# Feed-forward feature products with rounded and rest activations side by side, 512 columns per matmul

## The reference

```python
# block 1, each layer (D_FF = 4096)
h2 = rms_norm(x, mlp_norm_g[l])
x = x + jnp.square(jax.nn.relu(h2 @ w_up[l])) @ w_down[l]

# block 2, each layer, twice (ffn1 and ffn2; D_FF_2 = 2816)
def _swiglu(x, w1, w3, w2):
    return (jax.nn.silu(x @ w1) * (x @ w3)) @ w2
x = _layer_norm(a * x + 0.5 * _swiglu(x, ffn1_w1[l], ffn1_w3[l], ffn1_w2[l]), ln1_g[l], ln1_b[l])
```

## Time and profile before

| | us |
|---|---|
| median of 3 runs (lowest to highest) | 2394.6 (2394.44 to 2394.92) |
| the profiled execution | 2392.54 |
| its span, first to last instruction | 2390.8 |
| granted TensorE clock, mean | 0.990 |

### The profile page before, as it was taken

One profiled execution on the slowest core, in us unless ns is written; L12 is line 12 of the kernel. 1 busy time (PEld: TensorE's weight loads), 2 busy tenths in 40 slices (PEclk: granted clock), 3 DMA queues, 4 the chain that ended last, 5 costly groups with the idle time before them and its releaser, 6 DMA issues.

```text
span 2390.8 us, 38487 instructions
## 1 busy us (share of the span) xinstructions
PE 2311.5 (97%) x16084; PEld 2123.2 (89%) x16098; DVE 1353.6 (57%) x1782; ACT 1152.1 (48%) x1797; POOL 186.9 (8%) x191
## 2 busy tenths in 40 slices
PE   7999999999999999999999999999999999998998
PEld 6988988888998998799998889989988999897997
DVE  4556555646664545655566665465555555776454
ACT  4754544674553444545443544454444445355443
POOL 0001210001110210000003001111100000110110
PEclk9999999999999999999999999999999999999999
DMA  6324555432555655554533545565555444263554
GB/s 223 132 97 152 184 197 181 163 121 97 190 189 185 222 182 189 171 181 141 168 106 110 190 156 181 191 208 188 187 174 184 155 158 143 80 205 134 184 178 146
DMA packets 109005, 395.93 MB, mean 166 GB/s; under 512 B 12374, under 2 KB 12544, under 8 KB 108576
## 3 DMA queue, kind: packets, MB, share of 16 engines
q1 hardware_dynamic: 104400, 377.53, 47.7%
q0 software_dynamic: 4432, 15.93, 2.2%
HBM read 392.92 MB, written 1.05 MB: 165 GB/s over the span
## 4 chain that ended last, share of the span: by engine, by line
PE 89%; DVE 5%; ACT 3%; DMA 1%; issue 1%; SPq 0%; DVEq 0%; ACTq 0%
PE psum L390 80%; PE psum L805 2%; PE psum L771 2%; DVE w_low L347 2%; PE psum L707 2%; DMA ring<-in_weights 1%; PE psum L789 1%; ACT w_high L344 1%; ACT attn_p L887 1%; PE psum L1773 1%; DVE mx L831 1%; DVE xT_low L666 0%; PE psum L1113 0%; ACT xT_high L660 0%; PE psum L1101 0%
## 5 line engine op out<-in xcount | busy, mean ns | idle before, releaser
L347 DVE TENSOR_TENSOR w_low<-ring,w_high 128x1024 fp32r<-128x1024 f32 x704 | 863.5, 1255 | 577.3 <-ACT w_high L344 575.7
L344 ACT ACTIVATE w_high<-ring 128x1024 fp32r<-128x1024 f32 x704 | 718.0, 1052 | 302.1 <-DMA ring<-in_weights 301.5
L390 PE MATMUL psum<-xT_high,w_high 128*128 128x256 f32 x2976 | 848.0, 285 | 0.0
L390 PE MATMUL psum<-xT_low,w_high 128*128 128x256 f32 x2976 | 843.3, 283 | 0.0
L390 PE MATMUL psum<-xT_high,w_low 128*128 128x256 f32 x2976 | 843.2, 283 | 0.0
L390 PEld LDWEIGHTS psum<-xT_high,w_high 128*128 128x128 f32 x2976 | 572.6, 192 | 0.8
L390 PEld LDWEIGHTS psum<-xT_low,w_high 128*128 128x128 f32 x2976 | 572.6, 192 | 0.4
L390 PEld LDWEIGHTS psum<-xT_high,w_low 128*128 128x128 f32 x2976 | 572.3, 192 | 0.0
L390 PE MATMUL psum<-w_high,hidden 128*128 128x512 f32 x1216 | 376.6, 390 | 0.0
L390 PEld LDWEIGHTS psum<-w_high,hidden 128*128 128x128 f32 x1216 | 228.3, 188 | 47.1
L390 PE MATMUL psum<-w_low,hidden 128*128 128x512 f32 x608 | 236.6, 389 | 0.0
(11 more groups left out here) (233 smaller groups left out, 2196.0 us busy)
## 6 DMA issues: line engine op xcount, KB each, us to landing
ring<-in_weights SPq DMA_DIRECT2D x706, 512.0 KB, 3.7
pages<-in_affine POOLq DMA_DIRECT2D x16, 512.0 KB, 5.6
ring<-in_weights SPq DMA_DIRECT2D x8, 440.0 KB, 3.3
pages<-in_gains POOLq DMA_DIRECT2D x4, 512.0 KB, 5.1
pages<-in_mem POOLq DMA_DIRECT2D x2, 1024.0 KB, 6.1
ring<-in_weights SPq DMA_DIRECT2D x4, 384.0 KB, 3.1
x<-in_x_in SPq DMA_DIRECT2D x2, 512.0 KB, 4.3
pages<-in_rows POOLq DMA_DIRECT2D x2, 512.0 KB, 6.2
```

The lines of the kernel that those rows point to most:

```text
L344: eng.activation(high, raw, ACT.Copy).then_inc(self.flag("w_rounded").sem, 1)
L347: eng.tensor_tensor(self.w_low[:, piece % SLOTS, 0:width], raw, high.bitcast(F32), ALU.subtract).then_inc(self.flag("w_split").sem, 1)
L390: m = pe.matmul(out, a, b, start=(first and i == 0), stop=(last and i == len(pairs) - 1))
```

## The change

`xT_high` and `xT_low` become the two halves of one tensor `xT`, [128, 8, 2, 256], so that for each k the 512 columns "high beside low" lie in a row. A new routine, `gemm_beside`, makes one tile in one bank: for each k a 256-wide matmul of `w_low` with the high half into the first half of the bank, and a 512-wide matmul of `w_high` with both halves into the whole bank. The bank then holds two halves whose sum is the product. A new routine, `halves_added`, has VectorE add them with a reduction over pairs 256 elements apart, and mark the bank as drained.

Block 1: VectorE adds the halves into `attn_p`, then takes relu and square in one instruction, tile by tile, and a weight split follows each tile; ScalarE's relu goes away. Block 2: VectorE adds the halves of tile a, ScalarE takes Silu of the sum in place in SBUF, VectorE adds the halves of tile b and multiplies; one weight split follows each tile on both engines, ScalarE's ahead of its Silu. Each tile has a bank of its own, so there are twice as many groups.

```diff
@@ -232,8 +232,8 @@
         self.x = sb("x", [P, NT, D])
         self.xs = sb("xs", [P, NT, D])
 
-        self.xT_high = sb("xT_high", [P, KD, SEQ], F32R)
-        self.xT_low = sb("xT_low", [P, KD, SEQ], F32R)
+        self.xT = sb("xT", [P, KD, 2, SEQ], F32R)
+        self.xT_high, self.xT_low = self.xT[:, :, 0, :], self.xT[:, :, 1, :]
         self.w_high = sb("w_high", [P, SPLITS, PIECE], F32R)
 
 
@@ -491,6 +491,27 @@
                 self.used(l, stream, (tile[0], tile[1], k), m, self.flag("filled").last(l) if closing else None)
         self.piece_after[group] = self.piece_now
 
+    def gemm_beside(self, pe, l, stream, banks, group, act, kn, tile):
+
+
+
+        self.take_bank(pe, l, banks, group)
+        out = self.bank(banks, group)
+        for k in range(kn):
+            high, low = self.weight(pe, l, stream, (tile[0], tile[1], k))
+            act(k)
+            pe.matmul(out[:, 0:SEQ], low, self.xT_high[:, k, :], start=(k == 0), stop=False, skip_group_check=True)
+            m = pe.matmul(out, high, self.xT[:, k, :, :].rearrange("p x s -> p (x s)"), start=False,
+                          stop=(k == kn - 1), skip_group_check=True)
+            if k == kn - 1:
+                m.then_inc(*self.flag("filled").one())
+            self.used(l, stream, (tile[0], tile[1], k), m, self.flag("filled").last(l) if k == kn - 1 else None)
+        self.piece_after[group] = self.piece_now
+
+    def halves_added(self, dve, l, banks, key, out):
+        h = self.filled(dve, l, banks, key)
+        dve.tensor_reduce(out, h.rearrange("p (x s) -> p s x", x=2), AX, ALU.add).then_inc(*self.drained(banks, key))
+
     def input_parts(self, pe, l, j):
 
 
@@ -1002,9 +1023,10 @@
     for key, n in (("sbq", 2), ("sbk", 2), ("gate", 8), ("ysb", 4), ("ysw", 4)):
         for n in range(n):
             banks.add((key, n))
-    for key, n in (("out", 0), ("up", 16), ("down", 0)):
+    for key, n in (("out", 0), ("up", 32), ("down", 0)):
         for i in range(n):
-            banks.add(("upt", i) if i < 2 else (key, i))
+            if i not in (2, 3):
+                banks.add(("upt", i) if i < 2 else (key, i))
         if not n:
             for t in range(NT):
                 for i in range(2):
@@ -1178,8 +1200,8 @@
                         c.turn_bank(pe, f"first{i}", [
                             (c.psum[:, 4 + i, j * SEQ + t * P:j * SEQ + (t + 1) * P],
                              first[:, t, (2 * i + j) * P:(2 * i + j + 1) * P]) for j in range(2) for t in range(NT)])
-                c.gemm_features(pe, l, stream, banks, "up", ("up", n), xTf, KD,
-                                [("up", 2 * n - 4), ("up", 2 * n - 3)])
+                for i in (2 * n, 2 * n + 1):
+                    c.gemm_beside(pe, l, stream, banks, ("up", i), xTf, KD, ("up", i - 4))
             if l < DEPTH - 1:
                 after_down = lambda h, l=l: c.norm_turn(pe, l + 1, 0, 0, h, c.xs)
             else:
@@ -1296,12 +1318,10 @@
                     if n == 1:
                         after("upt")
                     continue
-                h = c.filled(act, l, banks, ("up", n))
-                act.wait_ge(*(c.flag("hidden_whole").at(l, n - 3) if n >= 4 else c.flag("first_whole").at(l, n - 1)))
-                act.activation(c.attn_p[:, n % 2, :], h, ACT.Relu).then_inc(*c.drained(banks, ("up", n)))
-                if n > 2:
-                    round_hidden(n - 1)
-                after(("up", n))
+                for i in (2 * n, 2 * n + 1):
+                    split(c.piece_after["up", i] + AHEAD)
+                    if i == 2 * n and n > 2:
+                        round_hidden(n - 1)
                 if n == 5:
                     for i in range(2):
                         c.part_out(act, l, "act", f"first{i}", 4 + i,
@@ -1468,12 +1488,15 @@
                     if n == 1:
                         after("upt")
                     continue
-                c.wait_drained(dve, l, banks, ("up", n))
-                if n >= 4:
-                    dve.wait_ge(*c.flag("hidden").at(l, n - 3))
-                dve.tensor_tensor(c.attn_pT[:, n % 2, :], c.attn_p[:, n % 2, :], c.attn_p[:, n % 2, :],
-                                  ALU.mult).then_inc(*c.flag("hidden_whole").one())
-                after(("up", n))
+                dve.wait_ge(*(c.flag("hidden").at(l, n - 3) if n >= 4 else c.flag("first_whole").at(l, n - 1)))
+                for i in (2 * n, 2 * n + 1):
+                    cut = slice(i % 2 * SEQ, (i % 2 + 1) * SEQ)
+                    c.halves_added(dve, l, banks, ("up", i), c.attn_p[:, n % 2, cut])
+                    c.wait_drained(dve, l, banks, ("up", i))
+                    sum_, whole = c.attn_p[:, n % 2, cut], c.attn_pT[:, n % 2, cut]
+                    dve.scalar_tensor_tensor(whole, sum_, 0.0, sum_, ALU.max, ALU.mult
+                                             ).then_inc(*c.flag("hidden_whole" if i % 2 else "dve_step").one())
+                    split(c.piece_after["up", i] + AHEAD)
                 if n == 5:
                     for i in range(2):
                         c.part_out(dve, l, "dve", f"first{i}", 4 + i,
@@ -1544,7 +1567,11 @@
 
     def ffn_groups(f):
         for n in range(KF2):
-            banks.add((f + "t", n) if n < 2 else (f, n))
+            if n < 2:
+                banks.add((f + "t", n))
+            else:
+                banks.add((f + "a", n))
+                banks.add((f + "b", n))
 
     def model_groups(key):
         for t in range(NT):
@@ -1690,7 +1717,8 @@
                             c.wait_drained(pe, l, banks, (f + "t", t))
                         c.turn_bank(pe, key, [(c.psum[:, 4, j * SEQ + t * P:j * SEQ + (t + 1) * P],
                                                first[:, t, j * P:(j + 1) * P]) for j in range(2) for t in range(NT)])
-                    c.gemm_features(pe, l, stream, banks, f, (f, n), xT, KD, [(f + "a", n), (f + "b", n)])
+                    for x in "ab":
+                        c.gemm_beside(pe, l, stream, banks, (f + x, n), xT, KD, (f + x, n))
                 c.gemm_model(pe, l, stream, banks, f + "d", c.hidden_parts(pe, l, KF2, 1, done, (key,)), KF2, then)
 
             def turn_features(key, src, bank=4, tiles=4):
@@ -1855,7 +1883,7 @@
                 split(c.piece_after[key] + AHEAD)
 
             def round_hidden(f, n):
-                c.wait_drained(act, l, banks, (f, n))
+                act.wait_ge(*c.flag("gated").at(l, (KF2 - 2 if f == "f2" else 0) + n - 1))
                 act.activation(c.hidden[KF2][0][:, n, :], gated[:, n % 4, :], ACT.Copy
                                ).then_inc(*c.flag("hidden_rounded").one())
 
@@ -1868,19 +1896,18 @@
                 for n in range(KF2):
                     if n == 4 and beside is not None:
                         beside()
-                    key = (f + "t", n) if n < 2 else (f, n)
-                    h = c.filled(act, l, banks, key)
-
-                    if n >= 4:
-                        c.wait_drained(act, l, banks, (f + "t", n - 4) if n < 6 else (f, n - 4))
-                    act.activation(silu[:, n % 4, :], h[:, 0:SEQ], ACT.Silu).then_inc(*c.flag("silu").one())
                     if n < 2:
+                        act.activation(silu[:, n % 4, :], c.filled(act, l, banks, (f + "t", n))[:, 0:SEQ], ACT.Silu
+                                       ).then_inc(*c.flag("silu").one())
                         if n == 1:
                             after(f + "t")
                         continue
+                    after((f + "a", n))
+                    c.wait_drained(act, l, banks, (f + "a", n))
+                    act.activation(silu[:, n % 4, :], silu[:, n % 4, :], ACT.Silu).then_inc(*c.flag("silu").one())
                     if n > 2:
                         round_hidden(f, n - 1)
-                    after((f, n))
+                    after((f + "b", n))
                     if n == 5:
                         c.part_out(act, l, "act", "first" + f[1], 4, *(x[:, 0:2, :] for x in c.hidden[KF2]))
                 round_hidden(f, KF2 - 1)
@@ -2064,9 +2091,9 @@
                 for n in range(KF2):
                     if f == "f1" and n == 6:
                         bias_low()
-                    dve.wait_ge(*c.flag("silu").at(l, done + n + 1))
-                    key = (f + "t", n) if n < 2 else (f, n)
+                    key = (f + "t", n)
                     if n < 2:
+                        dve.wait_ge(*c.flag("silu").at(l, done + n + 1))
                         dve.tensor_tensor(first[:, n, :], silu[:, n % 4, :], c.bank(banks, key)[:, SEQ:2 * SEQ], ALU.mult
                                           ).then_inc(*c.drained(banks, key))
                         if n == 1:
@@ -2074,9 +2101,16 @@
                         continue
                     if n >= 6:
                         dve.wait_ge(*c.flag("hidden").at(l, (KF2 - 2 if done else 0) + n - 5))
```

(40 more changed lines are left out.)

## The result

| | before | changed |
|---|---|---|
| median of 5 runs, us | 2394.6 (2393.65 to 2395.78) | 2382.68 (2376.36 to 2385.4) |
| ratio, 95% interval | | 0.9944 [0.9931, 0.9956] |
| the profiled execution, its span | 2392.54, 2390.8 | 2380.69, 2379.0 |
| granted clock, mean of the profiled execution | 0.990 | 0.988 |

The account below looks back on a forecast made before the run. TensorE's instruction stream was taken to bound the kernel. From the median 2394.6 us, 1728 k steps each 0.0133 us shorter take 23.0, with other costs taken as 0: 2371.6 us, range 2368 to 2380.

Parts of the forecast that it names:

- 0.1200 + 0.2267 = 0.3467 us: TensorE, per k of a changed tile: one 256-wide step plus one 512-wide step, instead of 0.3600 us, so 0.0133 less.
- 1728 x 0.0133 = 23.0 us: TensorE's whole gain: 216 tiles over two layers, 1728 k steps, each 0.0133 us shorter, 23.0 us.
- no extra at all: Best bound for TensorE's alternating stream: a wide matmul behind a narrow one pays nothing extra, 23 us more gain (2348.6).
- a load laid bare: Worst bound for TensorE's alternating stream: a weight load becomes visible; for the wide matmul's load, 102 us more, 2496 us.
- Rival 3: TensorE's mixed stream gives four fifths or more of the gain back as uneven steps: 2390 to 2395 us; chance 0.04.
- VectorE's cover: VectorE's added work stays hidden behind TensorE: in block 1 2.5 us per tile against 2.77, in block 2 4.4 against 5.55 per pair.
- Rival 1: VectorE becomes the bound of block 1, needing r + 1.82 us per tile: 2381 us at r = 1.4; chance 0.04.
- r = 0.95: Block 1: reduction time r in us from which VectorE needs more per tile than TensorE's 2.77 us.
- its lead: Block 1: VectorE's split is five pieces ahead, first read 11.1 us later, so some 8.5 us of lateness are hidden.
- Rival 2: TensorE: the load for the wide matmul isn't hidden, 0.419 us per k instead of 0.360, 2496 us; chance 0.05.
- "Nothing" for the boundaries: Tile and stage ends: doubled bank takings and "filled" increments priced at 0 (1.4 us otherwise), the down-projection's start not delayed.
- 2.5 ns over N/2.4: The skill page's warm gap between TensorE matmuls; by it the change would win only 4.3 us, a result within 0.2%.

Follow-up runs that it names:

- two k together: Changed kernel, with two 256-wide matmuls, then two 512-wide ones, for every two k: 2371.63 us, 0.991 of the kernel before; again on another chip 0.9913.
- three narrow: Changed kernel with TensorE's part undone, three 256-wide matmuls per k as before, all else kept: 2395.16 us, 1.0 of the kernel before.
- Eight k together: Changed kernel, with all eight 256-wide matmuls of a tile, then its eight 512-wide ones: 2373.96 us, 0.9911 of the kernel before.
- the alternating order: Changed kernel, with the order of the two matmuls turned around at every second k (narrow, wide, wide, narrow): 2374.26 us, 0.9909 of the kernel before.

## Why the prediction came out as it did

- **The direction and the mechanism were right.** TensorE's stream bounds the stage; two instructions for three shorten it; nothing else sets the end. With TensorE's part undone the ratio is 1.0 [0.9992, 1.0009].
- **The step that failed is the sum "0.1200 + 0.2267 = 0.3467 us" per k, and so the term 1728 x 0.0133 = 23.0 us.** It measured 17.8 in the first profile and 13.6 to 19.6 over four. I took steps from uniform streams and added them. The alternating stream has two paces, 0.3467 and 0.3533; each stage starts at the second, and passed to the first at the turning in 14 of 24. At 0.3533 only half of the 13.3 ns is won. Where the sum held, its terms didn't: 0.117 and 0.230, not 0.1200 and 0.2267; that they add up to the same isn't explained by any run. The prediction had said that this stream isn't in the trace, and yet gave as its bounds only no extra at all and a load laid bare. Rival 3 named uneven steps, but only with four fifths or more of the gain given back.
- **A term was missing: the clock.** 4.6 us in the profiled execution, 2.4 in the mean of all. The prediction treated the stages outside the change as fixed.
- **The two together make most of the miss.** With 5.2 us lost to the pace and 2.4 to 4.6 to the clock, 2371.6 becomes 2379.2 to 2381.4. The median was 2382.68, so over a microsecond stays open. The range ended at 2380, with room for 37% of the gain to be lost; 48% was. The changed kernel's single executions went from 2374.9 to 2386.9.
- **VectorE's cover was right, and larger than priced.** Reduction 0.69 taken, 0.689 measured; square 0.42 taken, 0.494 measured in block 1; split 1.34 taken, 1.216 measured. From start to start they are 2.2 us a tile, not 2.5. Rival 1 put everything beside the reduction at 1.82 us a tile; with an extra reduction it was 0.34 + 1.14 = 1.48, which is why its threshold of r = 0.95 was too low (by these figures, an estimate, 1.3). Where VectorE did bind, with two extra ones, its lead didn't save the lateness; it was paid behind the stage.
- **Rival 2 didn't happen.** No k cost more than before. Whether part of the uneven pace's 6.7 ns is a load laid bare no run shows: the recorded lengths of loads (0.187 to 0.189 us in the median) are alike at both paces.
- **"Nothing" for the boundaries held:** within a pace the step is unbroken across tiles.
- The Trainium skill's 2.5 ns over N/2.4 ("TensorE: Matmul & The Clock Gate", "Back-to-back issue gap"), by which the prediction worked out 4.3 us, doesn't agree with this trace: the means of all executions differ by 13.6 us.

Open is why the alternating stream has two steady paces and what in a break chooses one, beyond that a break is needed; and whether the lower clock belongs to the changed kernel. The falls lie outside the edited stages. One, at 144 us, came behind 4 us in which TensorE was busy for 2.28; others, as at 1997.5, came while its record has no gap. 0.9877 against 0.9887 is more than the scatter of the means. Yet two k together (0.9891 over 11 executions) and three narrow (0.9889 over 12), with the same work on the other engines, don't show it.

Two k together beats both kernels: 0.991 and 0.9913 of the kernel before in two sessions, where the changed kernel had 0.9941 to 0.9945 in four comparisons. Eight k together (0.9911) and the alternating order (0.9909) do as well, once each.

## What to carry to other kernels

Price a matmul by the distance between starts, and don't add steps from uniform streams to price a mixed one: run the mixed pattern once. Where a pattern of widths alternates strictly, try it in pairs (two narrow, two wide), which here gave one pace in every stage, 1.7 ns per k over the better of the two. A time that moves with the granted clock outside the change can hide or feign a few microseconds, so compare means over many executions, with their clocks.

## What the runs showed of the hardware

- One stream of loads and matmuls, 256 and 512 columns in turn, without a wait and at a granted clock of 1.00, ran at 0.3467 or at 0.3533 us per k. It kept to one to the end of a stage (272 k, 96 us, at the uneven pace), and not the same one in each execution.
- At 0.3467 each k had steps of 117 and 230 ns; at 0.3533 the steps repeated after three k: 113, 233, 117, 241, 120, 236 ns.
- Uniform streams had no such choice: 0.1200 us at 256 columns (kernel before, three narrow) and 0.2267 to 0.2270 at 512 (the down-projections of all fourteen profiles).
- After a change from 256 to 512 columns the steps took about five matmuls to settle from 0.234 to 0.227 us.
- VectorE adds two halves 256 apart, 512 elements from PSUM to 256, in 0.689 us; a reduction to two columns takes 0.68.
